# A chunked delta rule rescaled per token: keys times themselves instead of times scaled, transposed keys, and the level-3 copies placed ahead of the convolution's taps on ScalarE

## The reference

```python
# q, k l2-normalised, q * dk**-0.5; gam = cumsum(g) in a chunk; beta = sigmoid(...)
decay = exp(where(tril_incl, gam_i - gam_j, -inf))
kk    = k @ k.T
a_mat = where(tril_strict, beta_i * kk * decay, 0)
sol   = triangular_solve(eye + a_mat, [v * beta, k * beta * exp(gam)])   # u, w
qk    = where(tril_incl, (q @ k.T) * decay, 0)
def step(S, ...):                       # one chunk after the other
    v_new = u_c - w_c @ S
    o_c   = (q * exp(gam)) @ S + qk @ v_new
    S     = S * exp(gam_last) + (k * exp(gam_last - gam)).T @ v_new
```

## Time and profile before

| what | value |
|---|---|
| median of 3 runs | 2251.62 us (2249.67 to 2252.02) |
| the profiled execution | 2250.8 us |
| its span | 2249.0 us |
| TensorE busy | 98% of the span |
| weight loads, VectorE, ScalarE, GpSimd busy | 80%, 51%, 45%, 48% |
| chain that ended last, TensorE's share | 88% |
| mean DMA rate | 82 GB/s |

### The profile page before, as it was taken

The page is one execution under the profiler, slowest core; times in us unless marked ns, Lnnn a source line. Parts: engine busy times, 40 slices in busy tenths (PEclk is TensorE's granted clock), DMA queues, the critical chain, the costliest instruction groups (busy, mean ns, idle before and its releaser), DMA issues.

```text
span 2249.0 us, 35580 instructions
## 1 busy us (share of the span) xinstructions
PE 2200.1 (98%) x14164; PEld 1801.5 (80%) x14164; DVE 1145.2 (51%) x2171; ACT 1011.7 (45%) x2301; POOL 1080.1 (48%) x792
## 2 busy tenths in 40 slices
PE   8999999999999999999999999999999999999998
PEld 6777888788888888888877777878888888888886
DVE  7668875544352344440186678854445334444302
ACT  6546565555532433332365555655555233333222
POOL 4455535333354555554445355343334455555542
PEclk9999999999999999999999999999999999999999
DMA  4211221222233333333322121222222333333332
GB/s 154 71 53 53 62 58 55 74 75 75 71 97 95 94 99 95 98 99 95 88 80 76 49 57 58 57 58 75 76 75 76 98 98 91 97 99 96 96 99 89
DMA packets 98948, 183.39 MB, mean 82 GB/s; under 512 B 11104, under 2 KB 11360, under 8 KB 98784
## 3 DMA queue, kind: packets, MB, share of 16 engines
q1 hardware_dynamic: 98784, 181.12, 28.2%
HBM read 178.98 MB, written 2.10 MB: 81 GB/s over the span
## 4 chain that ended last, share of the span: by engine, by line
PE 88%; DVE 6%; ACT 3%; POOL 1%; issue 1%; DMA 0%; SPq 0%; DVEq 0%; ACTq 0%; POOLq 0%
PE bank L1633 86%; PE bank L1709 1%; PE bank L2021 1%; ACT w_hi L640 1%; POOL mt_even L581 1%; DVE ob_lo L1073 1%; DVE conv_acc L1076 1%; DVE inv L1073 1%; DVE bank L1073 0%; DVE z_act L1076 0%; DVE left L1287 0%; PE bank L1703 0%; ACT p_quad L651 0%; DMA residual<-x_t 0%; ACT conv_acc L651 0%
## 5 line engine op out<-in xcount | busy, mean ns | idle before, releaser
L543 POOL TENSOR_TENSOR w_lo<-w_raw,w_hi 128x512 fp32r<-128x512 f32 x668 | 930.4, 1414 | 1076.4 <-ACT w_hi L640 1076.4
L1633 PE MATMUL bank<-xn_hi,w_hi 128*128 128x512 f32 x1840 | 742.6, 404 | 5.0 <-DVE conv_acc L1076 4.2
L1633 PE MATMUL bank<-xn_hi,w_lo 128*128 128x512 f32 x1840 | 741.6, 403 | 0.0
L1633 PE MATMUL bank<-xn_lo,w_hi 128*128 128x512 f32 x1840 | 735.5, 400 | 0.0
L640 ACT ACTIVATE w_hi<-w_raw 128x512 fp32r<-128x512 f32 x668 | 384.9, 623 | 655.5 <-PE bank L1633 649.7
L1633 PEld LDWEIGHTS bank<-xn_hi,w_hi 128*128 128x128 f32 x1840 | 348.3, 189 | 81.0 <-DVE conv_acc L1076 7.1
L1633 PEld LDWEIGHTS bank<-xn_hi,w_lo 128*128 128x128 f32 x1840 | 348.5, 189 | 72.7 <-issue 5.8
L1633 PEld LDWEIGHTS bank<-xn_lo,w_hi 128*128 128x128 f32 x1840 | 348.4, 189 | 71.4 <-issue 2.2
L1073 DVE TENSOR_TENSOR residual<-residual,bank 128x512 f32<-128x512 f32 x32 | 21.9, 686 | 252.8 <-PE bank L1633 252.4
L1076 DVE SCALAR_TENSOR_TENSOR conv_acc<-bank,hconv,conv_acc 128x511 f32<-128x511 f32 x144 | 107.5, 747 | 66.4 <-ACT conv_acc L651 63.4
L1633 PE MATMUL bank<-mid_hi,w_hi 128*128 128x512 f32 x352 | 136.9, 389 | 0.0
(11 more groups left out here) (276 smaller groups left out, 3320.8 us busy)
## 6 DMA issues: line engine op xcount, KB each, us to landing
w_raw<-w_tiles SPq DMA_DIRECT2D x668, 256.0 KB, 2.6
residual<-x_t SPq DMA_DIRECT2D x4, 512.0 KB, 6.8
out_t<-normalised SPq DMA_DIRECT2D x8, 256.0 KB, 2.1
rope<-rope SPq DMA_DIRECT2D x2, 512.0 KB, 6.5
mats<-mats SPq DMA_DIRECT2D x1, 448.0 KB, 3.5
vecs_all<-vecs SPq DMA_DIRECT2D x1, 129.0 KB, 8.9
mats<-mats SPq DMA_DIRECT2D x1, 128.0 KB, 8.3
vecs_all<-vecs SPq DMA_DIRECT2D x1, 4.0 KB, 1.7
```

What stands on the lines that cost most here:

```text
L543: nc.gpsimd.tensor_tensor(w_lo[j][:], w_raw[j][:], w_hi[j][:].bitcast(F32), ALU.subtract).then_inc(s_lo, 1)
L1633: return nc.tensor.matmul(out, lhsT, rhs, start=start, stop=stop)
```

## The change

1. kk becomes the raw keys times themselves (`k_f` times `k_f`); k_b, kbT and the stage kbT with its 8 transpositions, ScalarE's evacuation of kbT and VectorE's two k_b instructions go.
2. The factors beta over norm come in per token elsewhere: a_t is made by scalar_tensor_tensor with fac, one instruction a chunk (8 a pair instead of 2); v_b is scaled by the norm (k_norm) instead of beta; v_new is scaled by fac as ScalarE copies it; the update of v_b multiplies by exp(gam) and has its sign turned, for which a small VectorE instruction makes -fac ("minus").
3. R reads the raw keys instead of kbg_t, whose two GpSimd instructions go. As the keys are now read until R3, they lie in two buffers that alternate by pair.
4. On ScalarE the level-3 copies into p_quad stand ahead of tile 1's tap.
5. FILL_WEIGHT, CONV_AT and topk_spots change. Products behind the stages, mid pair: start 12, kk 3, ot 2, qk 3, qt 2, sub 19, T0 2, P3 8, U3 9, P4 8, U4 9, P5 6, U5 2, P6 1, vt 2, U6 6, R/V/S/O 8/6/5/4, kt 6, gb 13; last pair: start 10, kk 3, ot 2, qk 2, qt 2, sub 18, T0 2, P3 8, U3 8, P4 8, U4 9, P5 8, U5 3, the others as before. In a mid pair tile 0 now ends in sub (before: ot), tile 1 in P3, tile 2 in U4, tile 3 in V0. In the last pair tile 1 ends in U3 (before: P3) and tile 2 with the last product of U4. On VectorE one half round of the top-k moves from U3 to U5, one from U5 to U6, and one from gb to ovar, ahead of rinvk.

```diff
 rinv = sb("rinv", [2, 2, NC])
+k_norm = sb("k_norm", [2, NC])
...
 q_f = per_head("q_f", 0)
-k_f = per_head("k_f", 1)
+k_of = [per_head("k_even", 1), per_head("k_odd", 9)]
 decay = per_head("decay", 5)
-k_b = per_head("k_b", 6)
+q_sq = per_head("q_sq", 6)
 mt = [per_head("mt_even", 8), per_head("mt_odd", 7)]
-kbg_t = per_head("kbg_t", 9)
 o_s = per_head("o_s", 12)
-kbT = per_head("kbT", 13)
...
-STAGES = (["start", "kbT", "kk", "ot", "qk", "qt", "sub", "T0_"]
+STAGES = (["start", "kk", "ot", "qk", "qt", "sub", "T0_"]
 head_a = steps("head_act", two("sqk") + ["ga0", "sqrtk", "ga1"] + two("exp"))
-head_v = steps("head_dve", ["hcol", "htot", "inv0", "vark", "rinvk", "fac"] + two("kb", "kd"))
+head_v = steps("head_dve", ["hcol", "htot", "inv0", "vark", "rinvk", "fac"] + two("kd") + ["minus"])
...
 gdn_p = steps("gdn_pe", [m for st in STAGES if st not in ("start", "ot", "T0_", "kt", "gb") for m in marks(st)])
-gdn_a = steps("gdn_act", two("kbT", "eg", "ztanh", "sqq") + ["qe"] + [f"P{L}_{r}" for L in QUADS for r in range(P // Q)]
+gdn_a = steps("gdn_act", two("eg", "ztanh", "sqq") + ["qe"] + [f"P{L}_{r}" for L in QUADS for r in range(P // Q)]
               + ["ovar", "orinv"] + two("osc"))
-gdn_g = steps("gdn_pool", two("dg", "mt3_", "mt4_", "kbg", "qd", "qm"))
+gdn_g = steps("gdn_pool", two("dg", "mt3_", "mt4_", "qd", "qm"))
...
-FILL_WEIGHT = {"mid": fill((12, 5, 4, 3, 3, 1, 19), (2, 8, 9, 4, 1), (1, 2, 6), (7, 6, 5, 4), (6, 4, 6, 13)),
-               "last": fill((9, 4, 4, 3, 2, 1, 18), (2, 8, 9, 7, 1), (1, 2, 6), (5, 5, 4, 4), (5, 12, 8, 0))}
-CONV_AT = {1: ("T0_", "T0_", "T0_", "P3_", "U3_"), 2: ("U4_", "U4_", "U4_", "P5_", "U5_"), 3: ("V0_", "V0_", "S0_", "O0_", "V1_"),
+FILL_WEIGHT = {"mid": fill((12, 3, 2, 3, 2, 19), (2, 8, 9, 6, 2), (1, 2, 6), (8, 6, 5, 4), (6, 4, 6, 13)),
+               "last": fill((10, 3, 2, 3, 2, 18), (2, 8, 9, 8, 3), (1, 2, 6), (5, 5, 4, 4), (5, 12, 8, 0))}
+CONV_AT = {1: ("U3_", "U3_", "U3_", "P4_", "P4_"), 2: ("U4_", "U4_", "U4_", "P5_", "U5_"), 3: ("V0_", "V0_", "S0_", "O0_", "V1_"),
...
         mask(FIRST + 1)
+        stages("start", "kk", "ot", "qk", "qt")
             pool.wait_ge(gdn_a.sem, gdn_a.after(t, f"eg{s}"))
-            nc.gpsimd.tensor_tensor(kbg_t[s][:], kbT[s][:], q_d[s][:], ALU.mult).then_inc(gdn_g.step(f"kbg{s}"), 1)
-        stages("start", "kbT", "kk", "ot", "qk", "qt")
-        for s in range(2):
-            pool.wait_ge(gdn_g.sem, gdn_g.after(t, f"kbg{s}"))
...
         act.wait_ge(head_v.sem, head_v.after(t, "vark"))
-        nc.scalar.activation(rinv[:, :, 1, :], rinv[:, :, 1, :], ACT.Sqrt).then_inc(head_a.step("sqrtk"), 1)
+        nc.scalar.activation(k_norm[:], rinv[:, :, 1, :], ACT.Sqrt).then_inc(head_a.step("sqrtk"), 1)
...
-        evac("kbT", kbT, bz)
...
             for c in range(NC):
-                last = nc.scalar.activation(k_b[s][:, c, :], chunks(by[s])[:, c, :], ACT.Square, accum_out=rinv[:, s, 0, c:c + 1])
+                last = nc.scalar.activation(q_sq[s][:, c, :], chunks(by[s])[:, c, :], ACT.Square, accum_out=rinv[:, s, 0, c:c + 1])
...
         last = P // Q - 1
-        tap_first = plan.ends["T0_"] if i < PAIRS - 1 else []
-        for m in tap_first:
-            tile_done(l, T0_GDN + 8 * (i + 1) + m)
-            front(l, i + 1, m, True, split_next=False)
             if L == QUADS[0]:
-                for m in tap_first:
-                    w_hi_after(l, T0_GDN + 8 * (i + 1) + m)
-                if not tap_first:
-                    stages("T0_")
+                stages("T0_")
...
             for c in range(NC):
-                last = copy(v_b[s][:, c, :], chunks(bx[s])[:, c, :], scale=hcol[:, s, 0, c:c + 1])
+                last = copy(v_b[s][:, c, :], chunks(bx[s])[:, c, :], scale=k_norm[:, s, c:c + 1])
                 act.wait_ge(gdn_p.sem, gdn_p.after(t, f"V{c}_{s}"))
-                copy(v_new[s][:], chunks(bx[s])[:, c, :]).then_inc(gdn_a.step(f"V{c}_{s}"), 1)
+                copy(v_new[s][:], chunks(bx[s])[:, c, :], scale=fac[:, s, 1 if c else 0, c:c + 1]).then_inc(gdn_a.step(f"V{c}_{s}"), 1)
...
                     dve.wait_ge(gdn_g.sem, gdn_g.after(ft - 1, f"qd{s}"))
-            dst = {"q": q_f, "k": k_f, "v": v_f}[n][s]
+            dst = {"q": q_f, "k": k_of[i % 2], "v": v_f}[n][s]
...
         dve.wait_ge(head_a.sem, head_a.after(t, "sqrtk"))
-        V.reciprocal(rinv[:, :, 1, :], rinv[:, :, 1, :]).then_inc(head_v.step("rinvk"), 1)
+        V.reciprocal(rinv[:, :, 1, :], k_norm[:]).then_inc(head_v.step("rinvk"), 1)
         dve.wait_ge(head_v.sem, head_v.after(t, "fac"))
-        for s in range(2):
-            tt_(k_b[s][:], chunks(bx[s]), over_free(fac[:, s, 0, :]), ALU.mult).then_inc(head_v.step(f"kb{s}"), 1)
             tt_(k_dec[s][:], chunks(bx[s]), over_free(fac[:, s, 2, :]), ALU.mult).then_inc(head_v.step(f"kd{s}"), 1)
+        V.tensor_scalar(fac[:, :, 1, :], fac[:, :, 0, :], -1.0, None, ALU.mult).then_inc(head_v.step("minus"), 1)
...
         halves = [(r, what) for r in range(first_round, first_round + ROUNDS_OF_PAIR[i]) for what in ("max", "take")]
-        topk_spots = (("U3_", "U5_", "O0_", "S1_", "R3_", "R3_", "R3_", "ovar", "gb", "gb") if tile_of is None
+        topk_spots = (("U5_", "U6_", "O0_", "S1_", "R3_", "R3_", "R3_", "ovar", "ovar", "gb") if tile_of is None
...
             dve.wait_ge(head_g.sem, head_g.after(t, f"dr{s}"))
-            tt_(a_t[s][:], chunks(bz[s]), decay[s][:], ALU.mult).then_inc(gdn_v.step(f"at{s}"), 1)
+            for c in range(NC):
+                last = stt(a_t[s][:, c, :], chunks(bz[s])[:, c, :], fac[:, s, 0, c:c + 1], decay[s][:, c, :], ALU.mult, ALU.mult)
+            last.then_inc(gdn_v.step(f"at{s}"), 1)
...
                     dve.wait_ge(gdn_p.sem, gdn_p.after(t, f"R{c}_{s}"))
-                    tt_(v_b[s][:, c, :], v_b[s][:, c, :], chunks(by[s])[:, c, :], ALU.subtract).then_inc(gdn_v.step(f"R{c}_{s}"), 1)
+                    stt(v_b[s][:, c, :], chunks(by[s])[:, c, :], cols[:, 2 * i + s, 1, c:c + 1], v_b[s][:, c, :], ALU.mult, ALU.subtract).then_inc(gdn_v.step(f"R{c}_{s}"), 1)
...
             pe.wait_ge(front_v.sem, front_v.after(t, f"silu{MADE[s, 'k']}"))
-            columns(bx[s], k_f[s]).then_inc(head_p.step(f"kt{s}"), 1)
+            columns(bx[s], k_of[i % 2][s]).then_inc(head_p.step(f"kt{s}"), 1)
...
         d.issue(dense_after["start"])
-        for s in range(2):
-            pe.wait_ge(head_v.sem, head_v.after(t, f"kb{s}"))
+        k_f = k_of[i % 2]
+        for s in range(2):
                 pe.wait_ge(gdn_v.sem, gdn_v.after(t - 1, f"osc{s}"))
-            columns(bz[s], k_b[s]).then_inc(gdn_p.step(f"kbT{s}"), 1)
-        d.issue(dense_after["kbT"])
-        for s in range(2):
-            pe.wait_ge(gdn_a.sem, gdn_a.after(t, f"kbT{s}"))
-            per_chunk(bz[s], k_f[s], kbT[s]).then_inc(gdn_p.step(f"kk{s}"), 1)
+            per_chunk(bz[s], k_f[s], k_f[s]).then_inc(gdn_p.step(f"kk{s}"), 1)
...
                     pe.wait_ge(gdn_v.sem, gdn_v.after(t, f"S{c - 1}_{s}"))
-                    mm(chunks(by[s])[:, c, :], kbg_t[s][:, c, :], state[s][(c - 1) % 2][:]).then_inc(gdn_p.step(f"R{c}_{s}"), 1)
+                    mm(chunks(by[s])[:, c, :], k_f[s][:, c, :], state[s][(c - 1) % 2][:]).then_inc(gdn_p.step(f"R{c}_{s}"), 1)
                 if c:
```

## The result

| | before | after |
|---|---|---|
| median of 4 runs | 2250.68 us (2249.67 to 2252.02) | 2235.34 us (2234.30 to 2236.51) |
| ratio | | 0.9932, 95% interval 0.9914 to 0.9949 |
| profiled execution, its span | 2250.8, 2249.0 us | 2236.51, 2234.7 us |

The change makes the kernel faster by 0.68% (0.51 to 0.86). The forecast was 2233, in a range of 2220 to 2245.

A forecast was written before the change was run, and what follows sets the result against it. It took TensorE, busy 98% of the span, as the bound, with the chain to sub as second limit. Terms -27.3 - 1.0 - 1.3 + 3.0 + 2.8 + 2.0 + 1.2 + 2.0 = -18.6 gave 2233 us, range 2220 to 2245.

The forecast's parts named there:

- Copies ahead of the tap: P3 to Y3 to P4 in mid pairs: no wait for p_quad and no clock drop, -17.1 and -10.2, -27.3 us.
- The reading from pair 3: Pair 3 has no tap before the copies, no wait and full clock; its 2.71 us P3 to Y3 prices the mid pairs.
- Rival D: At Y3: the copies' place changes nothing because something else holds Y3 as long; about 2251 us, chance 0.03.
- Transpositions gone, and the chain to sub: gb to P3: sub's input comes sooner, -1.0 us for pairs 1 and 2, -1.3 for pair 3.
- The walk of VectorE: Pair 1, VectorE's chain to sub: a_t starts at 186.5, packed_rows ends about 1.4 us sooner, at 192.0.
- The split's price: a_t on VectorE, 8 instructions instead of 2: +0.9 us a pair, bounds +0.4 to +1.2; 0.75 by the skill.
- Rival A: Ahead of sub: the transpositions count in full, -8.6 us, with no long wait in pair 0; 2219 us, chance 0.12.
- Pair 0: Before sub: a_t still waits for GpSimd's decay, TensorE stands some 3 us; +3.0 us over both layers.
- The clock's term: Behind sub of pair 0: lower clock after the long wait, 1.4 us in each layer, +2.8 in all.
- Rival B: Before sub: new waits lower the clock in all pairs, 8 to 14 us more; say 2244 us, chance 0.2.
- Y5 and the chunks: Late level-5 copies at Y5: +2.0 us mid pairs, +1.2 pair 3; waits for v_b in the chunks: +2.0.
- Rival C: The wait moves from Y3 to Y5, ACT 2.7 us late there, old wait and drop again; about 2258 us, chance 0.04.

The follow-up runs named there:

- order_only: Kernel before with only the level-3 copies ahead of tile 1's tap on ScalarE, tile 1's other steps at the change's stages: 2228.19 us; beside evened, 2229.39.
- stand_y3: Kernel after, with TensorE also waiting before Y3 of the mid pairs for tile 1's tap: 2252.90 us, ratio 1.0014.
- turned_back: Kernel after, with 8 transpositions of the keys a pair put back on TensorE ahead of kk, results unused: 2235.84 us, ratio 0.9940.
- decay_first: Kernel after, with GpSimd scaling decay in pair 0 of either layer ahead of w_lo of tile 7 instead of behind it: 2231.50 us, ratio 0.9916.
- whole_at: Kernel after, with a_t made by one instruction a head (2 instead of 8), a constant replacing the factor per token: 2231.14 us, ratio 0.9912.
- evened: decay_first with 3 more dense products behind start and 3 fewer behind P5 and U5: 2225.05 us, ratio 0.9885; again beside order_only, 2225.49.
- rescale_only: Kernel after, with ScalarE's order, tile 1's stages and the product plan of the kernel before (kbT's products put to start): 2249.27 us, ratio 0.9997.
- evened_turned: evened with 8 transpositions of the keys a pair put back on TensorE ahead of kk, results unused: 2225.59 us, ratio 0.9889.

## Why the prediction was right

**Copies ahead of the tap** (-27.3): -27.1. In order_only, where it stands alone, the same two stretches give -26.8, and P4 to P5 takes 2.6 back; its profiled execution is 23.0 us shorter, its median 21.4. The reading from pair 3, that at Y3 wait and lower clock go together, held, and stand_y3 shows it from the other side. Rival D is out.

**Transpositions gone, and the chain to sub.** The walk of VectorE was right to 0.1 us: reckoned from the first gb, a_t of pair 1 began at 186.5 (187.42 less 0.93 by which this pair began later), as forecast, its 8 instructions took 2.16 us (forecast 2.1) and packed_rows was ready at 191.9 (forecast 192.0). The split's price against the earlier trace rows, 2.16 - 1.29 = 0.87, is that of the row; the 0.75 that I made from the Trainium skill ("VectorE: DVE Perf Modes", TRN2 errata) is a little low, and at pair 1 of this trace the measurement decides. TensorE was ready 0.5 us later than I reckoned, so its wait there is 0.65 us and not 1.3; that changed no sum, as VectorE's side sets sub. Rival A, that the transpositions count in full, is refuted by turned_back: 0.5 of 8.6 in the time, 0.95 from gb to sub. That kbg_t's going frees VectorE, as the prediction has it beside the sum, no run shows by itself.

**Pair 0.** The wait of 2.95 us came as forecast (some 3), and the term of +3.0 for it was +3.1. The clock's term came out right by luck, by two errors that cancel: I took 1.4 us in each layer, and it was 2.8 in the first and 0 in the second. In stand_y3 the same two waits of 2.95 us have no such stretch, so another execution could have had 0 for this term. decay_first and whole_at show both causes of the wait, GpSimd's late decay and the split of a_t. Rival B, the lower clock behind every sub, did not come: behind waits of 0.3 to 0.7 us none is seen.

**Y5 and the chunks.** +2.0, +1.2 and +2.0 against +1.8, +0.9 and +2.1. The sums are right and the places only in part. At Y5 1.4 of the 1.8 us stand in the two pairs 0, and the other four mid pairs have 0 to 0.2 each, not 0.3. (The 2.2 us that I counted for P5's 0.69 and six products add up to 2.05, by which the term would have been 2.8.) In the chunks pairs 1 and 2 have 0.5 us each, pair 3 0.2 to 0.3, and pair 0 0.25 less than nothing, as two waits for v_new (2.1 us) have gone. TensorE's listed waits for v_b, the reason that I gave, grew by 0.7 us (2.4 to 3.1); that the rest is theirs too is not shown. Rival C needed a wait of 2.7 us at Y5; the longest is 0.6.

**P4 to P5** is the step that is missing: the sum has nothing there, and it cost 4.1 us, 3.4 less 0.5 of it by the idle times under "issue", in which, by the packets' rows, TensorE stands until instructions come (see the run with two products between Y and U). The trace of before has one such row, of 0.5 us, in the burst of level 4, and I priced nothing by it. With the 4.1 the sum would have been -14.5 against the measured -15.3; without them the forecast lies 2.3 us below the measured median (2233 against 2235.34).

**What the sum hid.** It was right as a whole, and showed from its terms that all beyond the first costs more than it gives: -18.6 against -27.3, so +8.7 with the cover left as it is. The runs agree (6 to 7 us), and evened shows why: 24 products stood behind P5 and U5 and were missing ahead of sub, where packed_rows was late in every pair (by 0.3 to 1.6 us in decay_first). Moved there, they fill 4.0 us of those waits, and 1.9 us of waits at Y5 go as well.

## What to carry to other kernels

When two engines arrive at a meeting point nearly together, work taken off one of them is worth only as much as the other gets sooner as well; price both chains before taking a change for a gain, and then move filler work to where the new waits are. An engine's queue should have what the bottleneck waits for in front of what merely frees a buffer: that exchange of two steps gave 21 us here, and the rearranged algebra around it by itself nothing. And look in the same profile for the pair, the layer or the tile that has the order you are about to make: its rows gave the two largest terms to 0.1 us.

## What the runs showed of the hardware

The lower clock doesn't follow from a wait's length alone; it goes with the place as well, and differs from one execution to the next. These are all waits of 1.6 to 3.3 us in the pairs of the 13 profiles:

| kernel | at Y3: waits, us | with a stretch at 0.50 | at sub of pair 0: waits, us | with it |
|---|---|---|---|---|
| before | 6, 2.6 to 3.0 | 6 | | |
| rescale_only | 6, 2.4 to 3.3 | 5 | 2, 1.8 | 0 |
| stand_y3 | 6, 1.7 to 1.8 | 4 | 2, 2.95 | 0 |
| after | | | 2, 2.95 | 1 |
| whole_at | | | 2, 2.6 | 0 |
| turned_back | | | 2, 2.1 | 1 |
| decay_first | | | 2, 1.6 | 0 |
| sum | 18 | 15 | 12 | 2 |

In rescale_only two waits of the same length at the same place, 2.41 us in pair 1 of the first layer and 2.40 in pair 1 of the second, had no stretch and one of 6.83 us (from 1316.71 on). And evened and evened_turned had one of 3.41 us each about P6 of a pair 0 (at 1236.28 and 138.17 us) with no wait over 0.93 us ahead of it in the pair, and a second profile of evened had none. At Y3 the wait stands between bursts of 32x32 products, at sub between dense ones and transpositions; that this is the difference was not tried. So a stretch at 0.50 may be priced as a chance with its rows; one of 3.41 us cost 1.0 to 1.6 us here, one of 6.83 us 1.9 to 2.8.

TensorE sits idle for 0.2 to 1.1 us (once 2.35) in or just ahead of bursts of 32x32 products, most often those of Y and U, 128 products of 32x32 by 32x16 at some 9 ns each. In 11 of the 13 profiles this is 2.4 to 4.6 us a run; in before it is 0.5, and with the bursts of Y and U split in two it is 1.1. All 84 of these idle times end 2.2 to 3.0 us behind the start of a 16 KB packet on the queue named instruction, and such packets start every 3.3 to 8 us in the bursts and every 20 to 31 us among dense products.
